# Output projections at 256 tokens: one 512-column matmul for the high weights, and VectorE adds the halves

## The reference

```
h = concat(meta (16 tokens), x (256 tokens))                  # 272 tokens
2 x:  h = h + 0.5 * (silu(n(h) @ w_gate) * (n(h) @ w_up)) @ w_down   # D_FF = 2816
      h = h + hybrid_mixer(n(h))           # stick-breaking attention and a convolution of 31 taps
      h = h + 0.5 * swiglu(n(h))           # n = RMS norm with a gain
h = rmsnorm(h)[16:]                                           # 256 tokens from here on
1 x:  h = h + 0.5 * swiglu(n(h)); h = h + diff_attention(n(h)); h = h + 0.5 * swiglu(n(h))
1 x:  h = h + 0.5 * swiglu(n(h)); h = h + retention(n(h));      h = h + 0.5 * swiglu(n(h))
```

## Time and profile before

| what | value |
|---|---|
| median of 3 runs | 2377.23 us (2376.45 to 2377.73) |
| profiled execution: span from first to last instruction | 2376.3 us |
| least that lies around the span, by the fastest run | 0.15 us |
| TensorE busy, of the span | 96% (2292.7 us) |
| VectorE busy | 65% (1549.1 us) |
| ScalarE busy | 51% (1200.9 us) |
| GpSimd busy | 14% (320.9 us) |
| DMA queue 1, share of 16 engines | 50.7% |
| mean granted TensorE clock | 0.981 |

### The profile page before, as it was taken

How to read it: one execution, slowest core, us unless ns; L and a number is a source line. 1 busy time by engine, 2 the same in 40 slices (tenths; PEclk the granted TensorE clock), 3 DMA queues, 4 the chain that set the end, 5 groups by cost and what they waited for, 6 DMA issues and landing times.

```text
span 2376.3 us, 48965 instructions
## 1 busy us (share of the span) xinstructions
PE 2292.7 (96%) x18446; PEld 2272.8 (96%) x18446; DVE 1549.1 (65%) x2314; ACT 1200.9 (51%) x1723; POOL 320.9 (14%) x362
## 2 busy tenths in 40 slices
PE   7999889999999998899998999989999999999999
PEld 7999888999999998799998999879999999999999
DVE  6655997665466569876656656876656656675663
ACT  5444656544444356565535545755535444464552
POOL 2001552300100126520011001020010010001000
PEclk9999998999999999899999999979999999999999
DMA  6565422555455553245654565325655565445563
GB/s 201 175 191 166 142 91 89 167 171 189 154 177 184 169 167 116 77 151 179 195 182 144 187 195 161 124 89 180 196 181 177 185 196 172 146 146 179 186 208 127
DMA packets 100942, 386.77 MB, mean 163 GB/s; under 512 B 11312, under 2 KB 13488, under 8 KB 100848
## 3 DMA queue, kind: packets, MB, share of 16 engines
q1 hardware_dynamic: 100128, 383.89, 50.7%
q0 software_dynamic: 432, 1.51, 0.2%
q10 hardware_dynamic: 288, 0.12, 0.0%
HBM read 384.42 MB, written 1.05 MB: 162 GB/s over the span
## 4 chain that ended last, share of the span: by engine, by line
PE 82%; DVE 8%; issue 5%; POOL 3%; ACT 2%; DMA 0%; ACTq 0%; POOLq 0%; DVEq 0%
PE bank L310 26%; PE bank L308 26%; PE bank L309 26%; DVE wlo L325 2%; POOL proj L1569 2%; DVE proj L1225 1%; ACT whi L318 1%; PE bank L672 1%; DVE qk L1248 1%; PE bank L798 0%; ACT dp L1019 0%; DVE dsc L1409 0%; PE bank L808 0%; DVE proj L1211 0%; PE bank L390 0%
## 5 line engine op out<-in xcount | busy, mean ns | idle before, releaser
L308 PE MATMUL bank<-u_hi,whi 128*128 128x256 f32 (+1 forms) x3968 | 1143.9, 288 | 23.5 <-DVE wlo L325 23.5
L310 PE MATMUL bank<-u_hi,wlo 128*128 128x256 f32 (+1 forms) x3968 | 1135.8, 286 | 0.0
L309 PE MATMUL bank<-u_lo,whi 128*128 128x256 f32 (+1 forms) x3968 | 1134.7, 286 | 0.0
L325 DVE TENSOR_TENSOR wlo<-raw,whi 128x1024 fp32r<-128x1024 f32 (+1 forms) x680 | 888.0, 1308 | 187.0 <-ACT whi L318 185.8
L318 ACT ACTIVATE whi<-raw 128x1024 fp32r<-128x1024 f32 (+1 forms) x680 | 746.3, 1111 | 252.2 <-PE bank L310 249.6
L308 PEld LDWEIGHTS bank<-u_hi,whi 128*128 128x128 f32 x3968 | 758.2, 191 | 25.9 <-DVE wlo L325 18.2
L310 PEld LDWEIGHTS bank<-u_hi,wlo 128*128 128x128 f32 x3968 | 758.1, 191 | 0.0
L309 PEld LDWEIGHTS bank<-u_lo,whi 128*128 128x128 f32 x3968 | 755.9, 190 | 0.8
L310 PE MATMUL bank<-hid_hi,wlo 128*128 128x256 f32 (+1 forms) x1408 | 400.6, 285 | 0.0
L308 PE MATMUL bank<-hid_hi,whi 128*128 128x256 f32 (+1 forms) x1408 | 399.4, 284 | 0.0
L309 PE MATMUL bank<-hid_lo,whi 128*128 128x256 f32 (+1 forms) x1408 | 398.1, 283 | 0.0
(11 more groups left out here) (231 smaller groups left out, 2194.8 us busy)
## 6 DMA issues: line engine op xcount, KB each, us to landing
raw<-w SPq DMA_DIRECT2D x552, 512.0 KB, 3.4
raw<-w SPq DMA_DIRECT2D x128, 704.0 KB, 4.7
proj<-xT SPq DMA_DIRECT2D x2, 544.0 KB, 5.2
outT<-h SPq DMA_DIRECT2D x8, 128.0 KB, 4.2
smask<-cst POOLq DMA_DIRECT2D x2, 216.0 KB, 2.7
consts<-cst POOLq DMA_DIRECT2D x1, 384.0 KB, 4.3
dist<-cst POOLq DMA_DIRECT2D x1, 192.0 KB, 3.8
rdist<-cst POOLq DMA_DIRECT2D x1, 192.0 KB, 2.8
```

The source lines that it names most:

```text
L308: pe.matmul(out, w_h, x_hi, start=first, stop=False)
L309: pe.matmul(out, w_h, x_lo, start=False, stop=False)
L310: return pe.matmul(out, w_l, x_hi, start=False, stop=last)
L325: dve.tensor_tensor(wlo[:, n % RING, 0:COLS[n]], raw[:, n % RING, 0:COLS[n]], whi[:, n % RING, 0:COLS[n]], ALU.subtract).then_inc(lo_ready, 1)
```

## The change

It concerns the `out_proj` calls with two panels per output tile and 256 tokens: phases 5, 7, 9, 10, 12 (feed-forward) and 11 (retention). High and low part of the input now lie side by side in one tensor (`hid`, `ry`). For each tile of input features the new `both_products` runs one matmul of 512 columns with the high weights (high part into columns 0 to 255 of the bank, low part into 256 to 511), and one of 256 columns with the low weights into columns 0 to 255. DVE then adds both halves of the bank into `h`, in two instructions with a semaphore (`h_half`) between them. The order of ACT's and DVE's splits around these adds changes too.

```
-            hid_hi = sb("hid_hi", [128, FT, T], f32r, area)
-            hid_lo = sb("hid_lo", [128, FT, T], f32r, area)
+            hid = sb("hid", [128, FT, 2, T], f32r, area)
...
-            ry_hi = sb("ry_hi", [128, 16, SEQ], f32r, area)
-            ry_lo = sb("ry_lo", [128, 16, SEQ], f32r, area)
+            ry = sb("ry", [128, 16, 2, SEQ], f32r, area)
...
+        def both_products(pe, out, slot, k, x, first, last):
+            w_h, w_l = whi[:, slot, k * 128:k * 128 + 128], wlo[:, slot, k * 128:k * 128 + 128]
+            pe.matmul(out[:, 0:2 * SEQ], w_h, x, start=first, stop=False, skip_group_check=True)
+            return pe.matmul(out[:, 0:SEQ], w_l, x[:, 0, :], start=False, stop=last, skip_group_check=True)
...   # PE, out_proj
-                                mm = products(pe, bank[4 + j % 2][:, 0:N], n % RING, k, *x(K),
-                                              K == 0, K == last)
+                                if per_tile == 2 and N == SEQ:
+                                    mm = both_products(pe, bank[4 + j % 2], n % RING, k, x(K), K == 0, K == last)
+                                else:
+                                    mm = products(pe, bank[4 + j % 2][:, 0:N], n % RING, k, x(K)[:, 0, :],
+                                                  x(K)[:, 1, :], K == 0, K == last)
...   # ACT, out_proj
+                    if first_col(y) > 0 and f < KD - 1:
+                        act_split(act, n0 + 2 * f + RING)
+                        act_update(act, y + 1, f)
+                        act_split(act, n0 + 2 * f + 1 + RING)
+                        continue
...   # DVE, out_proj
+                if per_tile == 2 and N == SEQ:
+                    halves = KD * sum(k in ("ffn", "rt") and first_col(i) > 0 for i, k in enumerate(PHASES[:y]))
+                    for f in range(KD):
+                        src = bank[4 + f % 2]
+                        dve.wait_ge(panel_used, n0 + 2 * (f + 1))
+                        dve.scalar_tensor_tensor(out=h[:, f, W], in0=src[:, SEQ:2 * SEQ], scalar=factor,
+                                                 in1=h[:, f, W], op0=ALU.mult, op1=ALU.add).then_inc(h_half, 1)
+                        if f < KD - 1:
+                            dve_split(dve, n0 + 2 * f + RING)
+                        dve.wait_ge(h_half, halves + f + 1)
+                        dve.scalar_tensor_tensor(out=h[:, f, W], in0=src[:, 0:SEQ], scalar=factor,
+                                                 in1=h[:, f, W], op0=ALU.mult, op1=ALU.add).then_inc(h_done, 1)
+                        if f == KD - 1:
+                            dve_split(dve, n0 + 2 * f + RING)
+                        dve_split(dve, n0 + 2 * f + 1 + RING)
+                        dve_update(dve, y + 1, f)
+                    return
```

More of the change, by code:

```diff
@@ L244, in build @@
         h_done, u_hi_ready, u_ready = sem("h_done"), sem("u_hi_ready"), sem("u_ready")
+        h_half = sem("h_half")
         sq_done, ssq_done = sem("sq_done"), sem("ssq_done")
@@ L488, in ffn @@
                     gate_up(it)
-                out_proj(y, b["P"] + 2 * FT, 2, HALF, lambda k: (hid_hi[:, k, W], hid_lo[:, k, W]),
+                out_proj(y, b["P"] + 2 * FT, 2, HALF, lambda k: hid[:, k, :, W],
                          hid_ready, b["F"] + FT, N)
@@ L639, in mix @@
                         mm.then_inc(panel_used, 1)
-                out_proj(y, P + 44, 1, KD, lambda k: (qk[:, k, W2], qk[:, KD + k, W2]), m_ready,
+                out_proj(y, P + 44, 1, KD, lambda k: qk[:, k::KD, W2], m_ready,
                          KD * (l + 1), N2)
@@ L810, in rt @@
                             mm.then_inc(r_osum, 1)
-                out_proj(y, b["P"] + 48, 2, KD, lambda k: (ry_hi[:, k, :], ry_lo[:, k, :]), r_y_ready,
+                out_proj(y, b["P"] + 48, 2, KD, lambda k: ry[:, k, :, :], r_y_ready,
                          16, SEQ, lag=6)
@@ L867, in pair @@
                         act.wait_ge(prod_done, F + 1 + 2 * it)
-                        act.activation(hid_hi[:, f, W], pr[:, p, W], ACT.Copy).then_inc(hid_hi_ready, 1)
+                        act.activation(hid[:, f, 0, W], pr[:, p, W], ACT.Copy).then_inc(hid_hi_ready, 1)
                 act.preload_act_table_set(SILU)
@@ L1060, in gated_hi @@
                     act.wait_ge(r_p_done, j + 1)
-                    act.activation(ry_hi[:, j, :], rp[:, j % 2, :], ACT.Copy).then_inc(r_y_hi, 1)
+                    act.activation(ry[:, j, 0, :], rp[:, j % 2, :], ACT.Copy).then_inc(r_y_hi, 1)
                 for t in range(RT_HEADS + 2):
@@ L1180, in tile @@
                     dve.wait_ge(hid_hi_ready, F + 1 + it2)
-                    dve.tensor_tensor(hid_lo[:, f, W], pr[:, p, W], hid_hi[:, f, W], ALU.subtract)\
+                    dve.tensor_tensor(hid[:, f, 1, W], pr[:, p, W], hid[:, f, 0, W], ALU.subtract)\
                        .then_inc(hid_ready, 1)
@@ L1447, in gated_lo @@
                     dve.wait_ge(r_y_hi, j + 1)
[L1448 removed]
+                    dve.tensor_tensor(ry[:, j, 1, :], rp[:, j % 2, :], ry[:, j, 0, :], ALU.subtract).then_inc(r_y_ready, 1)
                 for t in range(RT_HEADS + 2):
```

## The result

The changed kernel takes 2388.56 us (median of 4 runs, 2386.95 to 2390.08) against 2377.48 us before (4 runs): ratio 1.0043, 95% interval 1.0029 to 1.0058. It is slower by 0.43%, 11 us; 2387.6 was predicted.

The account below looks back on a forecast made before the run. PE's matmul number and pitch were taken to bound the output projections. Matmuls -10.5, passages +13.6, last addition +0.45 and clock +6.8 sum to +10.4 us: 2377.2 becomes 2387.6 us, range 2375 to 2397.

Parts of the forecast that it names:

- The passage: Behind phases 5, 7, 9, 10, 11: PE waits for `u_lo` behind two splits, 4 x 2.9 + 2.0 = 13.6 us.
- the longer way through two norms: Behind phase 5: the chain to the second norm's matmul moves 2.0 us; PE's 2.9 us wait is partly absorbed.
- The clock: Behind the new PE stalls: granted clock falls to 0.50 at four of five, 1.7 us each, 6.8 us lost.
- The matmuls: Output projections, 1008 steps: one 512-column and one 256-column matmul replace three of 256, saving 10.5 us.
- the mean of two estimates: Saving per projection step: mean of the near estimates 9 and 12 ns, 10.4 ns; ends 0 and 22 us in all.
- my line through 256 and 272 columns: Price of a 512-column matmul in the projections: straight line gives 228 ns, saving 9 ns a step.
- a column a cycle: Price of a 512-column matmul in the projections: 118.5 + 107 = 225 ns, saving 12 ns a step.
- Rival (c): Projections: 512 columns stream in 215 ns, saving 22 us, stalls leave the clock alone; 2369 us, chance 0.07.
- Rival (b): Projections: the matmul's fixed part goes with the columns, so no saving; 2398 us, chance 0.12.
- Rival (a): Passages between phases: the stalls come, but the clock stays at 1.00; 2380.8 us, chance 0.2.
- Inside the projections: VectorE and ScalarE work for f < 7 stays hidden behind the matmuls; retention tile 5.2 to 5.4 of 5.5 us; no cost.
- rival (d): Retention: DVE falls behind, each of 7 tiles waits some 0.3 us, 2 us more; 2390 us, chance 0.03.

Follow-up runs that it names:

- `u_lo` first: Changed kernel, but at f = 7 VectorE writes `u_lo` directly behind the second addition, ahead of both splits; 2371.9 us against 2378.65 before, ratio 0.9971.
- `u_lo` in the middle: Changed kernel, but at f = 7 VectorE writes `u_lo` between the two splits; 2382.79 us against 2378.65 before, ratio 1.0014.
- order only: Kernel before, three products and one addition, with only `u_lo` moved behind the splits at f = 7; 2390.61 us against 2378.65, ratio 1.0049.

## Why the prediction was right, step by step

- **The passage: right.** Predicted was `u_lo` ready at 5.17 us behind the first addition and a stall of 2.9 us; measured 5.16 us (1787.71 to 1792.87) and 2.98. Putting that one instruction back removed all five stalls, moving it in the kernel before produced them. Behind phase 5 I counted 2.0 us for the longer way through two norms; that stretch grew by 2.3 us against before and by 3.0 against the run with `u_lo` first, a clock drop included. That part of the wait is absorbed there is not shown by itself: with `u_lo` in the middle, without a drop, it grew by 1.9 us for a stall of 1.85.
- **The clock: right in kind and nearly in number.** I counted four drops at 1.7 us, three came. 9 to 10 grew by 4.64 us, 11 to 12, without a drop, by 3.08: the drop cost 1.6 us.
- **The matmuls: the mechanism right, the term mis-sized.** The step that failed is the mean of two estimates, 10.4 ns a step, 10.5 us in all. Measured: 5.67 us in the projections, with the 0.45 us of the last addition in them, so 6.1 us. 512 columns take about 232 ns, 4 ns above my line through 256 and 272 columns, and 7 above a column a cycle. The line went through two measurements that may differ in more than the number of columns: placing the same data differently moved a step of three matmuls of 256 columns between 353 and 360 ns, which is as much as the effect I was reading off. Of 6.1 us, 0.37 a feed-forward, 1.9 us together, are the layout's; 4.3 are the matmul's, 3.4 ns a step in the feed-forwards and 10 in the retention. With `u_lo` first the projections' 5.7 us are what is left of the whole change; the median is 6.8 us lower, and the profile has most of the rest ahead of phase 5, where two profiles of one kernel differ by up to 2.7 us.
- **Rival (c), 215 ns for 512 columns, falls**, and with it the formula of the Trainium skill, "TensorE: Matmul & The Clock Gate", section "Back-to-back issue gap": 216 ns there, 231.7 ns here for 512 columns in a row. The page gives the formula for a single matmul without a budget for the weight load, and here each matmul brings one. The measurement decides. Rival (b), pitch proportional to the columns, was nearer than I gave it: 256, 384 and 512 columns at 118, 178 and 232 ns. It fails as a result, since there was a saving. Rival (a), no drop, is refuted by two profiles.
- **Inside the projections: right.** No PE wait stands there in the changed kernel; the retention's tile takes 5.6 us and rival (d) did not come.
- **What cancelled.** The forecast lay 1 us off the median, and 1.5 off by the traces, because two errors met, and that is luck: 4.4 us too much saved at the matmuls, and some 5 us too much at the passages (20.4 predicted, 15.25 measured). Of these about 1.7 are the fourth drop. Another 2.4 were given back in the differential attention: the stretch 7 to 9 has a stall of 2.98 us and grew by 0.60. Before, the clock there was 0.71 on average, after it was 0.91, by these stretches (before, then after):

```profile
1551.00:1592.40 41.40, 31.85 (x173) 28.74 (x172) 24.09 (x52) 19.92 (x47) 6.79 (x7) 0.71 0.18 53
```

```profile
1553.00:1592.40 39.40, 28.52 (x196) 25.74 (x195) 24.51 (x54) 19.56 (x47) 5.62 (x6) 0.91 0.16 55
```

In all three profiles with stalls of 3.0 or 2.5 us this stretch grew by much less than its stall (0.60 and 0.74 us in the changed kernel, 0.37 with order only), with `u_lo` in the middle by 1.3 and 1.4 us for 1.85. That a shift of the start by some microseconds moves these drops is my reading; it was not tested.

## What to carry to other kernels

When a change touches the tail of a stage, write down the order of each in-order engine there and ask of every moved instruction who waits for it: 2.4 us of splits ahead of one 0.48 us instruction cost more than twice what 1008 shorter steps gave. Ask it for the last iteration apart from the others, because there the cover of the next tile's work is gone. A saving read off a difference of a few ns between two stages needs a check that the stages differ in nothing else.

## What the runs showed of the hardware

- The pitch (start to start) of fp32r matmuls with a weight load each is close to proportional to the columns, 118 ns at 256, 178 at 384, 232 at 512. Merging two into one saved 3.4 ns (feed-forwards) and 10 ns (retention) of a step of 353 and 360 ns.
- For the same shapes and count, a step of three 256-column matmuls took 353, 355, 355.5, 356.7 or 360 ns. Changing only where the moving operand lies moved it from 355.5 to 353, from 355 to 356.7 and from 360 to 356.6. Rows of 272 instead of 256 elements took 3 ns off in one place. No rule was found.
- A stall of 3 us in dense work cost 1.6 us more than itself when the clock fell behind it, which it did in 6 of 10 cases; behind stalls of 1.85 us it fell in none of ten.
